# The sample tile's 32 gather steps and its eight retrievals at the end of the step order instead of between the two pairs of prompt tiles

## The reference

```python
q = (hb @ w_peer_q).reshape(PEER_BLOCK, PEER_HEADS, 2, PEER_HALF)
s = jnp.einsum('thpc,hpkc->thpk', q, sub_keys)
s1, i1 = lax.top_k(s[:, :, 0], PEER_TOPK)
s2, i2 = lax.top_k(s[:, :, 1], PEER_TOPK)
cand = s1[..., :, None] + s2[..., None, :]          # 16 x 16
top_s, top_c = lax.top_k(cand, PEER_TOPK)           # 16 of 256
idx = e1 * N_KEYS + e2                              # 16384 experts
g = jax.nn.softmax(top_s)
a = einsum('td,tkd->tk', hb, expert_u[idx])
wgt = g * gelu(a)
out = einsum('tk,tkd->td', wgt, expert_v[idx])
```

## Time and profile before

| | |
|---|---|
| median of 3 runs | 2536.16 us (2514.55 to 2541.18) |
| profiled execution | 2534.09 us |
| its span | 2532.3 us |
| busy share of the span | PE 65%, DVE 61%, ACT 34%, POOL 30% |
| dots | first at 618.4 us, number 272 at 1744.7, number 512 at 2439.8, last at 2524.7 |
| HBM traffic | 755 MB, 298 GB/s over the span |

### The profile page before, as it was taken

One profiled execution on the slowest core, in us unless ns is written; L12 is line 12 of the kernel. 1 busy time (PEld: TensorE's weight loads), 2 busy tenths in 40 slices (PEclk: granted clock), 3 DMA queues, 4 the chain that ended last, 5 costly groups with the idle time before them and its releaser, 6 DMA issues.

```text
span 2532.3 us, 30152 instructions
## 1 busy us (share of the span) xinstructions
PE 1657.3 (65%) x9960; PEld 736.1 (29%) x9960; DVE 1535.6 (61%) x3742; ACT 869.8 (34%) x2357; POOL 751.6 (30%) x714
## 2 busy tenths in 40 slices
PE   7888899996777767665687778776333334334343
PEld 3455555443322333332333323232000000000000
DVE  1488743123647788686887866536566566566664
ACT  2122223012445243342444553334233333233332
POOL 0343100001233323222232223224344434244442
PEclk9999999998889958677787889898555555555555
DMA  4323445656898858679797889899999999999998
GB/s 191 107 86 101 167 150 227 247 197 230 322 381 340 322 214 303 240 271 327 263 355 262 339 335 397 314 408 404 338 386 375 372 372 381 343 387 381 398 382 339
DMA packets 173320, 756.80 MB, mean 299 GB/s; under 512 B 60228, under 2 KB 86076, under 8 KB 93404
## 3 DMA queue, kind: packets, MB, share of 16 engines
q0 software_dynamic: 78336, 570.46, 58.1%
q1 hardware_dynamic: 94828, 184.42, 20.4%
HBM read 734.57 MB, written 20.50 MB: 298 GB/s over the span
## 4 chain that ended last, share of the span: by engine, by line
DVE 24%; DMA 22%; SPq 8%; PE 7%; issue 4%; ACT 2%; POOL 0%; DVEq 0%; ACTq 0%; POOLq 0%
DMA ring<-in_expert_uv,pick 10%; DVE ring L1702 7%; SPq L773 7%; DMA sco<-x_sc 6%; DMA pick<-ig 6%; PE z L1087 4%; DVE yT L1618 2%; PE acc L1191 2%; DVE cand L1657 1%; DVE e L1658 1%; DVE ti L1626 1%; DVE ti L1629 1%; DVE sco L1627 1%; DVE cand L1655 1%; DVE tv L1628 1%
## 5 line engine op out<-in xcount | busy, mean ns | idle before, releaser
L1016 POOL DMA_INDIRECT ring<-in_expert_uv,pick x544 | 630.6, 1159 | 1141.6 <-PE acc L1191 914.0
L1702 DVE CUSTOM_DVE_ANT_0 ring<-ring,rep 128x1024 f32<-128x1024 f32 x544 | 659.0, 1223 | 394.8 <-DMA ring<-in_expert_uv,pick 372.4
L1191 PE MATMUL acc<-ring,fold 128*32 128x256 f32 x4352 | 478.0, 528 | 600.2 <-ACT fold L1350 596.7
L1087 PE MATMUL z<-wts,hT 128*128 128x384 f32 (+1 forms) x1408 | 637.3, 590 | 62.4 <-DVE tmp L1742 42.3
L1346 ACT ACTIVATE gel<-dots 128x1 f32<-128x1 f32 x544 | 110.0, 202 | 893.1 <-DVE dots L1702 892.5
L1191 PEld LDWEIGHTS acc<-ring,fold 128*32 128x32 f32 x4352 | 103.2, 127 | 968.5 <-ACT fold L1350 894.3
L1087 PEld LDWEIGHTS z<-wts,hT 128*128 128x128 f32 x1408 | 266.0, 204 | 327.3 <-issue 252.9
L1618 DVE SCALAR_TENSOR_TENSOR yT<-uT,vec,yT 128x256 f32<-128x256 f32 x480 | 218.0, 500 | 3.9 <-DVE nm L1777 0.3
L1087 PE MATMUL z<-wts,yT 128*128 128x512 f32 x384 | 191.3, 632 | 20.5 <-ACT yT L1511 17.3
L1350 ACT ACTIVATE fold<-cst,wgt 128x32 f32<-128x32 f32 x544 | 174.8, 321 | 17.7
L1348 ACT ACTIVATE wgt<-gel,pick 128x1 f32<-128x1 f32 x544 | 160.3, 295 | 17.6
(11 more groups left out here) (199 smaller groups left out, 1673.8 us busy)
## 6 DMA issues: line engine op xcount, KB each, us to landing
wts<-in_w_qkv SPq DMA_DIRECT2D x24, 1536.0 KB, 7.4
wts<-in_w_glu SPq DMA_DIRECT2D x8, 2048.0 KB, 12.1
wts<-in_w_gate SPq DMA_DIRECT2D x8, 2048.0 KB, 10.9
wts<-in_w_wq SPq DMA_DIRECT2D x8, 2048.0 KB, 11.2
ring<-in_k_cache SPq DMA_DIRECT2D x8, 1536.0 KB, 9.6
ring<-in_v_cache SPq DMA_DIRECT2D x8, 1536.0 KB, 8.4
rep<-x_h SPq DMA_DIRECT2D x68, 128.0 KB, 15.4
pick<-ig SPq DMA_DIRECT2D x544, 1.0 KB
```

The costliest lines, as they stand in the source:

```text
L1016: eng.indirect_dma_start(ring[:, i % RING, :], None, a["expert_uv"], bass.IndirectOffsetOnAxis(picks(i, 0).bitcast(U32), 0)).then_inc(row_ ...
L1087: mm = eng.matmul(bank[:, 0:w], of[:, k, :], rows[:, k, :], start=(k == 0), stop=(k == depth - 1))
L1191: mm = eng.matmul(acc[b][SUB * c:SUB * (c + 1), col:col + 256], fold[:, i % 4, :], ring[:, i % RING, D + 256 * c:D + 256 * (c + 1)], start ...
L1702: eng.tensor_tensor_reduce(u, u, rep[:, j, :], 1.0, 0.0, ALU.mult, ALU.add, dots[:, i % 4:i % 4 + 1]).then_inc(dot_ready, 1)
```

## The change

The order of the tiles in the steps becomes 0, 1, 2, 3, sample. The sample tile's eight retrievals stood at steps 8, 40, ... 232 (every 32), eight steps behind one prompt item and eight ahead of the next; now they stand at 264, 296, ... 488, again so between prompt items. Its 32 gather steps were 256 to 287 and are now 512 to 543. Tiles 2 and 3 move up by 32 steps, to 256 and 384, and the limit for the steps beside the dense part falls from 272 to 240, with the same ticks; 304 steps then remain behind the last tick. Nothing is added or removed: 544 steps, 40 retrievals, the same transfers.

```diff
-STEP_TILES = (0, 1, NT, 2, 3)
+STEP_TILES = (0, 1, 2, 3, NT)
...
     for t in STEP_TILES:
         for h in range(PH):
-            at = 8 + 32 * h if t == NT else BASE[t] - 16 + 16 * h
+            at = BASE[2] + 8 + 32 * h if t == NT else BASE[t] - 16 + 16 * h
             out.append((-1 if (t, h) == (0, 0) else at, t, h))
     return sorted(out)
```

## The result

The changed kernel takes 2545.91 us (median of 10, 2534.71 to 2550.21) against 2526.39 for the kernel before in the same 10 rounds (2514.55 to 2541.18): a ratio of 1.0077, 95% interval 1.0049 to 1.0105. The range was stated in us, on a kernel before of 2534; as a ratio its lower end is 2550/2534.1 = 1.0063, and 1.0077 lies just inside it. The size is off either way: 20 us in the medians and 9 in the profiled executions, where the sum gave 94.

A forecast was written before the change was run, and what follows sets the result against it. Bounds: DVE mid-way beside the dense work; in the tail, bandwidth and the chain retrieval, spread, gather. Sum: -120 + 88 + 98 + 8 + 20 = +94 on 2534.1, stated as 2630 us, range 2550 to 2705.

The forecast's parts named there:

- part 1: Overlapped stretch from dot 0 to the end of the dense work: 32 steps and 8 retrievals leave, a 120 us gain.
- B: Dots 48 to 192, beside the dense work: DVE sets the pace, so 4 retrievals and 18 steps fewer save 66 us.
- their 56 us: DVE's waits for scores ahead of prompt retrievals beside the dense work: 56 us, taken as unchanged.
- Part 3: Tail: sample retrievals delay the chain through SP's order, 14 us for each of seven pairs (98), 8 for the eighth.
- Part 2: Tail: 32 more steps behind the dense work at 2.74 us each, +88 us.
- Part 4: Tile changes without the sample tile between: 5 us more at 256 and 15 at 512, bounds together 5 to 40.
- Short landings: Score loads in the tail land in 1.9 us, so sample items delay it by 28 us: +11, 2545 us; chance 0.08.
- Bandwidth alone sets the tail: Sample items fit in DVE's idle time in the tail, all 169 us of DVE's relief is time: 2468 us; chance 0.11.
- Little relief, full delay: PE and waits between engines limit the overlapped part's relief to 80 us, sample items delay by 133: 2703 us; chance 0.18.

## Why the prediction was wrong, and where it was right

The two differences, -198 in the window and +199 in the tail, split by the runs so:

| | forecast | measured | from |
|---|---|---|---|
| window: 32 steps fewer | -53 | -106.4 | 1061.2 to 954.8 |
| window: eight retrievals fewer, without their waits | with the next line -67 | -36.3 | 954.8 to 918.5 |
| window: waits for scores | | -55.4 | 1126.3 to 1061.2, less 918.5 to 928.2 |
| tail: 32 steps more | +88 | +79.3 | 785.1 to 864.4 |
| tail: tile changes, with the retrievals' own work | +20 | +19.9 | 864.4 to 884.3 |
| tail: sample items and SP's order | +106 | +102.7 | 884.3 to 987.0 |

(Two amounts are in no line: early score loads took 2.5 us from the tail of the kernel before, 787.6 to 785.1, and the 8.0 lies before the first dot. The split goes by the order of the edits; in another order the same parts could come out otherwise.)

**The step that failed is part 1.** Its direction was right, its size was not: 120 us forecast, at most 169, and 198 measured. Those 78 us are most of the 85 between the sum's +94 and the +9 of the profiled executions. Two terms of it:

- *"B: 4 x 10.8 + 18 x 1.3 = 66 us, counted in full, since DVE is the pace."* DVE was 78% busy there with few waits for rows (17.9 us), and I took that for the pace. Then a step was worth its dot, 1.3 us, and a retrieval its full 10.8. Measured, a step was worth 3.3 and a retrieval 4.5. Halving the dots showed why the reading fails: 142 us less work on DVE, 31 us less time. Taken away for all 272 steps, half the bytes gave 82 us, half the dots 31 and the gelu 20, so none of these alone makes the price of a whole step, and even their sum, 133 us or 0.5 a step, is far from it. PE was left out of this by the folds' overlap and remains a rival. That a step takes from several engines at once and from the hand-overs between them would fit, but is argued, not shown.
- *"Prompt items are 16 steps apart, and I leave their 56 us as they are."* They fell to 14.7. Moving only the limit had the same effect (8.5 ahead of prompt items), so it comes with fewer steps in each tick, not with the sample items gone. I have no run that shows why.

**Part 3, the term that decided the sign, held.** 98 + 8 forecast, 102.7 measured, by changing nothing but the order of SP's queue. Within it sizes were off and cancelled, so the nearness of the sum is partly luck. In the pair shown above, the sample's scores took 11.3 us to land, not 9. The next prompt head's took 4.5, not 10: the stall had drained the DMA queues (their share was 0.34 from 1853 to 1870, 0.92 in the 15 us before). Prompt to prompt was 58.5 us (1816.0 to 1874.5) where I had 63. But the second half of the pair gave nothing back, 46.0 us to the next prompt retrieval (1920.5), where I had counted on 39. The Trainium skill's fixed cost of about 2 us for a DMA (DMA: Bandwidth & Descriptors, Latency and other measured facts) would, by an estimate with 2 us for each landing, have made this term 28 us. Even with drained queues the loads of the tail that I read took 4.5 to 5.0 us.

**Part 2** was near: 79 for 88. **Part 4**, 20 forecast, has the mechanism right and a size that is not settled: 19.9 by the table, together with the retrievals' own work, but 8 in the tails and 14 in the medians of the two kernels that differ in the order of the tiles alone, and 11 by the order of the slots. At 512 the trace shows both forecast stalls, DVE waiting for the reloaded slot and then for rows that PE's bank wait had held up:

```profile
2455.33 1.22 DVE L1703 CUSTOM_DVE_ANT_0 ring<-ring,rep 128x1024 f32<-128x1024 f32 x1 [10.38 <-DMA rep<-x_h]
...
2471.14 1.23 DVE L1703 CUSTOM_DVE_ANT_0 ring<-ring,rep 128x1024 f32<-128x1024 f32 x1 [7.73 <-DMA ring<-in_expert_uv,pick]
```

**The rivals.** "Short landings" came nearest in time (2545), by luck: its relief of 120 was 198 and its delay of 28 was 103, and the errors cancelled. "Bandwidth alone sets the tail" is refuted by the half-bytes run (37.2 us a head) and by the early score loads; its other half, the full 169 us of relief, was too small rather than too large. "Little relief, full delay" is refuted by the window.

**What stays open.** Why the first 16 of the 32 steps are worth 4.2 us each and the next ones 2.2 to 2.4. The granted clock goes with it: the 15.8 us by which the dense matmuls are shorter are 1.0 of the 4.2 us, and 6.9 us are 0.4 of the next 2.4. If all of that were time of the window, 3.2 against 2.0 would be left. The runs with the longer lead speak against the wait of PE for folds as the cause; a limit by transfers alone is not in accord with the 82 us that half of the bytes gave; PE's own work was not taken away in any run that kept its steps; an alignment of the steps with the dense ticks would fit but wasn't tried. The price of a step there is thus measured, not explained.

## What to carry to other kernels

- Before moving work between two stages, measure the exchange rate: change only the number of steps that stand in each (one constant here). A busy share of 78% on an in-order engine doesn't make its instruction time the price of a step; here that was too low by a factor of 2.5 for the last 32 steps. The rate also changes: below 240 steps a step less brought 1.9 us in the window and cost 3.1 in the tail.
- When a run takes work away from an engine to test whether it sets the pace, read in the trace that the engine's busy time really fell. Half of the fold matmuls took 2 us of 814 from PE, and the unchanged window said nothing.
- When work is moved on an in-order queue that others depend on, follow the queue's order and not only the work: eight retrievals cost the tail next to nothing by themselves and 103 us by standing behind a spread of 16 DMAs. The remedy was to issue the small load as soon as its buffer is free, ahead of the wait: a ratio of 0.955 to the kernel before, with the changed order and a slot order that fits it, and 0.964 in the old order with 256 steps.

## What the runs showed of the hardware that I had not expected

- The last 31 steps of the changed kernel, with no retrieval among them, took 79.2 us, 2.55 each; before, with one retrieval and its spread among them, they took 84.9, 2.74 each. From dot 520 on, behind the stall, the changed kernel took 57.8 us for 23 steps, 2.51 each. So the 2.74 that I used for the bandwidth of a step is not a floor.
- A score load of 128 KB landed in 4.5 us right behind a stall of DVE and in 11.2 to 22.8 us in the full tail, while a load of 32 KB took 11.3 us with the DMA engines full. Size is not what makes the difference.
- Eight records of fold matmuls take 0.40 us each in the median and 0.70 us together; four of them take 0.69.
- The mean granted TensorE clock beside the dense work rose from 0.85 to 0.89 when 32 steps were taken out, and the same dense matmuls took 602 us instead of 625.
